# Seven products of block sums in place of eight in the up projections of two feed-forwards, one hidden tile at a time

## The reference

```
# first block: h is (1024 tokens, 1024), ffn_up (1024, 2 * 2816)
p = h @ ffn_up                       # columns 0..2815 gate, the rest up
p = causal_conv3(p) + bias           # over tokens, all 5632 channels
x = x + rms((gelu(gate) * up) @ ffn_down)
# second block: w_up (1024, 2 * 2816), the gate u alone is convolved
u, v = z @ w_up
x = x + rms((silu(causal_conv3(u) + bias) * v) @ w_down)
```

## Time and profile before

| | |
|---|---|
| device time, median of 3 runs | 3082.59 us |
| profiled execution: its span, first to last instruction | 3080.9 us |
| PE busy | 3025.3 us, 98% |
| DVE busy | 1515.0 us, 49% |
| ACT busy | 1043.1 us, 34% |
| POOL busy | 740.9 us, 24% |
| matmuls | 22236 |
| first feed-forward's up products | 655 to 1346 us of the span |
| second feed-forward's | 2335 to 3029 us |

### The profile page before, as it was taken

How to read it: one execution, slowest core, us unless ns; L and a number is a source line. 1 busy time by engine, 2 the same in 40 slices (tenths; PEclk the granted TensorE clock), 3 DMA queues, 4 the chain that set the end, 5 groups by cost and what they waited for, 6 DMA issues and landing times. The chain is left out here.

```text
span 3080.9 us, 52491 instructions
## 1 busy us (share of the span) xinstructions
PE 3025.3 (98%) x22236; PEld 2625.0 (85%) x22236; DVE 1515.0 (49%) x2126; ACT 1043.1 (34%) x1503; POOL 740.9 (24%) x629
## 2 busy tenths in 40 slices
PE   8999999999999999999999999999999999999999
PEld 6788888787888878879999999899978888888887
DVE  6898864544333344356365665663423333333333
ACT  3133444432222221143455656563322112111112
POOL 0003322312122221121343343441211222221121
PEclk9999999999999999999999999999999999999999
...
DMA packets 198610, 173.28 MB, mean 56 GB/s; under 512 B 8830, under 2 KB 180438, under 8 KB 198038
## 3 DMA queue, kind: packets, MB, share of 16 engines
...
## 5 line engine op out<-in xcount | busy, mean ns | idle before, releaser
L2260 POOL TENSOR_TENSOR ffn_w_lo<-ffn_raw,ffn_w_hi 128x1024 fp32r<-128x1024 f32 x86 | 207.2, 2409 | 1034.9 <-ACT ffn_w_hi L2419 776.6
L2281 PE MATMUL ffn_out<-blk_hi,ffn_w_hi 128*128 128x512 f32 (+1 forms) x1592 | 446.9, 368 | 1.2 <-PEq L118 1.2
L2281 PE MATMUL ffn_out<-blk_hi,ffn_w_lo 128*128 128x512 f32 (+1 forms) x1592 | 446.2, 368 | 0.0
L2281 PE MATMUL ffn_out<-blk_lo,ffn_w_hi 128*128 128x512 f32 (+1 forms) x1592 | 445.9, 367 | 0.0
L3348 PE MATMUL mix_e<-blk_hi,mix_w_hi 128*128 128x348 f32 (+3 forms) x1056 | 346.5, 328 | 3.6 <-DVE blk_lo L2538 2.9
L3348 PE MATMUL mix_e<-blk_lo,mix_w_hi 128*128 128x348 f32 (+3 forms) x1056 | 339.6, 322 | 0.0
L3348 PE MATMUL mix_e<-blk_hi,mix_w_lo 128*128 128x348 f32 (+3 forms) x1056 | 338.6, 321 | 0.0
L2281 PEld LDWEIGHTS ffn_out<-blk_hi,ffn_w_hi 128*128 128x128 f32 x1592 | 289.7, 189 | 46.1 <-issue 2.1
L2281 PEld LDWEIGHTS ffn_out<-blk_hi,ffn_w_lo 128*128 128x128 f32 x1592 | 289.5, 188 | 44.0
L2281 PEld LDWEIGHTS ffn_out<-blk_lo,ffn_w_hi 128*128 128x128 f32 x1592 | 289.8, 188 | 43.6
L2419 ACT ACTIVATE ffn_w_hi<-ffn_raw 128x1024 fp32r<-128x1024 f32 x44 | 46.7, 1062 | 722.5 <-PE ffn_out L2281 722.5
...
## 6 DMA issues: line engine op xcount, KB each, us to landing
...
```

What stands on the lines that cost most here:

```text
L2260: G.by(nc.gpsimd.tensor_tensor(w_lo[i % 2][:], raw[i % 2][:], w_hi[i % 2][:], ALU.subtract), f"lo{i}")
L2281: mm = nc.tensor.matmul(o, a[i % 2][:, k, :], b[:, k, first:first + n], start=k == 0 and part == 0, stop=k == KD - 1 and part == 2)
```

## The change

Both feed-forwards, with one hidden tile (a gate tile and its up tile) per turn, 22 turns.

The up product of one hidden tile is a 2x2x2 product of blocks. The weights: A11 and A21 are rows 0 to 511 of depth of the gate's and of the up side's 128 columns, A12 and A22 rows 512 to 1023. The features: B11 and B21 are those rows for the first 512 tokens, B12 and B22 for the last 512. Tiles 0 and 1 (`PLAIN = 2`) are made as before, as plain products. While they run, four sums of features are made, each in high and low parts (`t_sums`, `t_split_hi`, `t_split_lo`; 4 slices of depth, for each 10 DVE operations in a chain):

The diff, cut:

```diff
+LOW = 3584
+PLAIN = 2
...
-    groups = F1 // P // 2
+    groups = F1 // P
...
+    CHUNKS = [DOWN[0:4], DOWN[4:8], DOWN[8:12], DOWN[12:16]]
+    act_names = ["dhi", "x", "hi_P7", "hid_hi", "hi_P3", "hi_P4", "c11", "hi_P2", "hi_P1", "hi_P6", "convg", "gelu", "hi_P5"]
+    pool_names = ["dlo", "lo_P7", "lo_P3", "lo_P4", "lo_P2", "S1", "S3", "lo_P1", "S2", "S4", "lo_P6", "lo_P5"]
+    dve_names = ["hid", "u2", "hid_lo"] + CHUNKS[0] + ["u3", "c22"] + CHUNKS[1] + ["c12", "down8", "tapga", "down9",
+                 "down10", "tapgb", "down11", "c21", "down12", "down13"]
...
+    pe_names = ["P1", "P6", "P5", "P2"] + CHUNKS[0] + ["P7"] + CHUNKS[1] + ["P3"] + CHUNKS[2] + ["P4"] + CHUNKS[3]
...
         def turns(eng, turn):
 
-            turn(0, 0, True, False)
-            with eng.Fori(0, (groups - 1) // 2 - 1) as h:
-                turn(2 * h + 1, 1, True, True)
-                turn(2 * h + 2, 0, True, True)
-            turn(groups - 2, (groups - 2) % 2, True, True)
-            turn(groups - 1, (groups - 1) % 2, True, True, True)
+            turn(FIRST_FAST, FIRST_FAST % 2, True, extra=True)
+            with eng.Fori(0, (ALONE - FIRST_FAST) // 2) as h:
+                turn(2 * h + (FIRST_FAST + 1), (FIRST_FAST + 1) % 2, True)
+                turn(2 * h + (FIRST_FAST + 2), FIRST_FAST % 2, True)
+            for g in range(ALONE + 1, groups):
+                turn(g, g % 2, False, last=g == LAST)
...
         def gpsimd(pool):
...
+            def next_group(g, j):
+                split_lo(j, "P2", 3, R12)
+                pool.wait_ge(landed["21"], (g + 2) * 16)
+                pool.wait_ge(landed["22"], (g + 2) * 16)
+                G.by(tt(S1, R21, R22, ALU.add), "S1")
+                pool.wait_ge(landed["11"], (g + 2) * 16)
+                G.wait(pool, j, "S1")
+                G.by(tt(R21, R11, R21, ALU.subtract), "S3")
+                split_lo(j, "P1", 0, R11)
+                G.wait(pool, j, "lo_P1")
+                G.by(tt(R11, S1, R11, ALU.subtract), "S2")
+                G.wait(pool, j, "S2")
+                G.by(tt(R12, R12, R11, ALU.subtract), "S4")
...
+            for n in range(1, 2 * PLAIN):
+                plain_split_lo(pool, n)
+                for m in range(4):
+                    t_split_lo(pool, tt, n - 1, m)
...
         def tensor(pe):
...
+                G.wait(pe, j, "lo_P1", back=1)
+                A.wait(pe, j, "c11", back=1)
...
+                M.by(gate_product(0, 0, True), "P1")
+                G.wait(pe, j, "lo_P6", back=1)
+                V.wait(pe, j, "c21", back=1)
+                if extra:
+                    pe.wait_ge(t_lo_ready, 4 * half)
+                    pe.wait_ge(plain_tap, 2 * PLAIN)
+                M.by(block_product(1, block_t(T2_), [bank_b], True), "P6")
+                G.wait(pe, j, "lo_P5", back=1)
+                V.wait(pe, j, "c12", back=1)
+                M.by(block_product(2, block_t(T1), [bank_c], True), "P5")
+                G.wait(pe, j, "lo_P2", back=1)
+                A.wait(pe, j, "x")
+                M.by(gate_product(3, half, False), "P2")
+                downs(0)
+                G.wait(pe, j, "lo_P7")
+                V.wait(pe, j, "u2")
+                M.by(block_product(0, block_t(T3), [bank_b], False), "P7")
+                downs(1)
+                G.wait(pe, j, "lo_P3")
+                V.wait(pe, j, "c22")
+                M.by(block_product(1, b22, [bank_c], False), "P3")
+                downs(2)
+                G.wait(pe, j, "lo_P4")
+                V.wait(pe, j, "u3")
+                M.by(block_product(2, block_t(T4), [bank_b], False), "P4")
+                downs(3)
+                if extra:
+                    pe.wait_ge(extra_lo, 1)
+                    pe.wait_ge(plain_hid_lo, 2)
+                    V.wait(pe, j, DOWN[-1])
...
         def scalar(act):
...
+            plain_split_hi(act, 1)
+            act.wait_ge(eps_ready, 1)
+            plain_conv(0)
+            t_split_hi(0)
+            plain_split_hi(act, 2)
+            plain_activate(0)
+            t_split_hi(1)
+            if not second:
+                plain_conv(1)
+            plain_hidden_hi(0)
+            plain_split_hi(act, 3)
+            t_split_hi(2)
...
         def vector(dve):
...
+                step(t1, h12, h11, ALU.subtract)
+                step(t1, t1, l12, ALU.add)
+                step(t1, t1, l11, ALU.subtract)
...
+            t_sums(0)
+            plain_taps(0)
+            t_sums(1)
+            plain_taps(1)
+            plain_hidden(0)
+            plain_hidden_lo(0)
+            t_sums(2)
+            plain_taps(2)
+            t_sums(3)
+            for m in range(4):
+                t_split_lo(dve, vec.tensor_tensor, 3, m)
+            plain_taps(3)
+            plain_hidden(1)
+            plain_hidden_lo(1)
...
-    nc = bacc.Bacc("TRN2", target_bir_lowering=False, num_devices=1)
+    nc = bacc.Bacc("TRN2", target_bir_lowering=False, num_devices=1, dynamic_dma_scratch_size=1024)
```

817 lines of the change are left out of this document (554 added, 263 removed).

## The result

The changed kernel takes 3067.45 us, the median of four runs (3065.7 to 3068.67), beside 3082.36 for the kernel before on the same chip: a ratio of 0.9946, 95% interval 0.9932 to 0.996. It is 0.5% faster, 15 us by the medians, where 26.6 were forecast; the time lies in the stated range.

A forecast was written before the change was run, and what follows sets the result against it. TensorE, busy 98% of the span, was taken as the bound. Gain 127.4 us less losses of 31.7 + 23.7 + 12.5 + 10.1 + 4.8 + 18.4 = 101.2 left 26.2 off 3082.6: 3056 us, own range 3035 to 3080, wider range 3010 to 3092.

The forecast's parts named there:

- What goes: Last 20 hidden tiles of each feed-forward: 54.5 us and 60 us of products plus 12.9 us of waits saved, 127.4 us.
- The start: Making the feature sums, with DVE and POOL blocking each other, stalls PE 31.7 us in the first feed-forward, 23.7 second.
- rival 1: In the starts nothing blocks and sums run at 0.72 us a step: 3000 us; chance 0.17.
- The clock: After PE's idle gaps the granted clock falls to 0.50; five gaps that count, 12.5 us lost.
- Case 4: Half clock lasts through the starts and last tiles, some 10 us per feed-forward: 3076 us; chance 0.10.
- The third tile: Extra down tiles behind its turn wait for DVE's down15 and POOL's split: 6.5 us first, 3.6 second, 10.1 together.
- The steady turn: PE has 30.0 us a turn; DVE's tight path costs 0.3 us over 16 turns, 4.8 us first, 0 second.
- rival 2: DVE's path runs late before down0 in the first feed-forward, some 3 us a turn, 48 us: 3104; chance 0.13.
- rival 3: Narrow matmuls pay their weight load, 67 us: 3123 us; chance 0.03.
- The last three tiles and the end: P3's waits without downs, 5 us each side plus 2; last weight splits 5 us first, 1.4 second: 18.4 us.
- The sum: Whole kernel: losses 101.2 us against gain 127.4, net 26.2 us, forecast 3056 us.

The follow-up runs named there:

- Experiment 1: Changed kernel with the 12 low parts of the sums in each start made by VectorE instead of GpSimd; 3061.57 us, ratio to before 0.9928.
- 5: Changed kernel with sums in 8 steps per slice instead of 10, three additions into PSUM, and product 3's weights split earlier; 3036.5 us, ratio to before 0.9845.
- experiment 2: Changed kernel with ScalarE splitting plain product 3's weights ahead of the convolution write and hidden tile 0's high part; 3065.76 us, ratio to before 0.994.
- experiment 4: Changed kernel with TensorE doing filler matmuls into an unused bank while it waits in each start; 3065.67 us, ratio to before 0.9941.
- Experiment 7: Changed kernel with tile 2's second set of down products begun in parts, as banks become free; 3059.85 us, ratio to before 0.9923.
- Experiment 6: Changed kernel with P7 ahead of P2 in the last three turns, skipped names signalled by matmuls, last down weights split earlier; 3074.69 us, ratio to before 0.9974.
- 9: Changed kernel with ScalarE's convg ahead of hi_P6 in every turn and skipped names signalled by the products' matmuls; 3065.03 us, ratio to before 0.9938.

## Why the prediction was right, and by what it was off
**What goes.** Forecast 127.4 us. By the turns it is (33.38 - 30.26) x 20 = 62.4 in the first and (33.48 - 30.51) x 20 = 59.4 in the second: 121.8. The products were sized right (54.5 and 60). The term that was too large is the 12.9 us of waits from the earlier trace rows: they are waits of weight loads, partly behind matmuls still under way. What PE itself lost is 66.77 us less 288 x 0.229 (the pace of the changed kernel's turns), 0.8 us in a turn of two tiles: some 8 in the first feed-forward, and next to nothing in the second. (the earlier trace rows has 45.27 us of up products, not 45.0; with half of it the second's 60 us would be 63, farther from what came.)

**The start.** Forecast 31.7 and 23.7 us; measured 78.1 - 48 = 30 and 70.8 - 49 = 22. P6 was forecast at 734.4 us in the first and stood at 732.75. Mechanism and size held: the four slices of ten steps took 12.4, 12.3, 12.7 and 11.4 us, single steps up to 2.8. But the 30 us are not all idle time, as the forecast's 31.7 were. The four waits add up to 22.6 us (16.8 in the second), and the rest is products that ran at the lower clock between them, 6.6 and 4.8 us longer than at full clock. Since DVE's chain set P6, they only filled time in which PE would have waited. By either count the start lies within the 15 to 45 us that the prediction allows. Experiment 1 shows the blocking, 5 that blocking and number of steps together set P6. What the earlier trace rows and the Trainium skill's page "SBUF — State Buffer", section "Who interferes with whom", say of two SBUF inputs beside GpSimd holds here: 0.69 us with one input in PSUM, and up to 2.8 with both in SBUF. The forecast wrote four waits and added them; experiment 2 shows that only their sum means something. (The prediction's "second case below", where nothing blocks, is its rival 1.)

**The clock.** Forecast 12.5 us. PE started every 0.43 us instead of every 0.23 at a granted clock of 0.50, the lower of its two levels, for 5.7 us behind P6 in the first (733.00 above), and likewise behind the second P6, the two third tiles' waits, the last P6 and the end of the first. Over full clock the starts behind these six gaps come to 2.7, 2.6, 1.8, 2.7, 1.4 and 1.6 us: 12.8. So the term was sized right, with a sixth gap that was not among the five. What it is worth is another matter: experiment 4 removed the 5.3 us behind the two P6 and gave back only 1.8, since in the first feed-forward the next wait took the rest. Case 4, a half clock through the whole start, did not come: behind the two longest waits of the first start PE was slow for 6.4 and 5.7 us, and full clock stood between, here behind product 3, whose slow stretch ends at 707.8.
```profile
702.00:703.00 1.00, 1.00 (x4) 0.81 (x3) 0.97 (x2) 0.00 (x0) 0.00 (x0) 0.50 0.34 88
709.00:710.00 1.00, 1.00 (x6) 0.84 (x5) 0.96 (x2) 0.13 (x1) 0.79 (x1) 1.00 0.00 0
```

**The third tile.** Forecast 6.5 and 3.6 us, measured 5.65 and 3.62. Experiment 7 leaves 2.2 and 2.0 of it.

**The steady turn.** Forecast 4.8 us in the first; measured nothing, since PE is busy all the time (a window of the changed kernel, PE's busy time second):
```profile
sum 480.00, PE 480.00 PEld 393.39 DVE 353.11 ACT 167.56 POOL 289.47; mean PE 480.00 PEld 393.39 DVE 353.11 ACT 167.56 POOL 289.47
```
That is 780 to 1260 us, and the pace is 132 matmuls in 30.26 us, 0.229 each. The slack is there, rival 2's 3 us a turn did not come, nor did rival 3: turns of the second with 48 narrow matmuls take 30.51, forecast 30.5.

**The last three tiles and the end.** This is the step that failed most: forecast 18.4 us, measured some 22 in the first and 11 in the second. PE's three turns took 74.7 us in the first (1265.6 to 1340.3), where 252 matmuls at 0.229 make 57.7, and 68.7 in the second (2944.9 to 3013.6) instead of 58.4: 17 us, 1.4 of them the lower clock counted above, and 10.3. The ends add 6.3 and 0.8. I wrote "1.6 us per tile" for P3, which is right (1.60), plus 2 us for chains that "nearly fill the 20.7 us". They overfill it: 22.7, 23.9 and 28.1 us in the first. At the end of the first, where I had 5 us, one wait for the last down weights' low part alone took 5.62:
```profile
1355.39 1.03 PE L2547 MATMUL ffn_out<-top_ident,ffn_meta 16*128 16x16 f32 x8 [5.62 <-POOL ffn_T L2410]
```
Between products 0.3 us are added wherever TensorE's sequencer passes the names of absent down products; that was not foreseen. Experiment 6 shows that taking P3's wait and those of 0.3 away does not shorten these turns; 9 shortened them by 5.0 and 2.2 us, and P6 still waits. So it is a chain through ACT, POOL and DVE that sets them; which link of it is longest stays open.

**The sum.** 30 + 22 + 12.8 + 9.3 + 0 + 33 = 107 us of losses against a gain of 121.8: some 15 us, where the spans differ by 14.8. Forecast were 101.2 and 127.4. Each side was off by some 6 us, both against the kernel. Inside the losses the last tiles were 15 us over their term; that the whole is off by only 6 is partly luck, since the starts came 3 and the steady turns 5 us under theirs.
